# A recurrent section on quarters of the TensorE array: state steps, inside products and turned keys laid out anew

## What is computed

```
state = state * w_t + (state @ a_t) b_t^T + v_t k_t^T      # 64 x 64 per head
y_t   = state @ r_t
```

## Time and profile before

| | |
|---|---|
| median of 3 runs | 2911.92 us (2911.47 to 2911.98) |
| span of the profiled execution | 2909.9 us |
| TensorE busy | 2892.3 us, 99% |
| TensorE weight loads | 2423.8 us, 83% |
| VectorE busy | 1572.7 us, 54% |
| ScalarE busy | 1103.5 us, 38% |
| GpSimd busy | 1584.3 us, 54% |

### The profile page before, as it was taken

One profiled execution on the slowest core, in us unless ns is written; L12 is line 12 of the kernel. 1 busy time (PEld: TensorE's weight loads), 2 busy tenths in 40 slices (PEclk: granted clock), 3 DMA queues, 4 the chain that ended last, 5 costly groups with the idle time before them and its releaser, 6 DMA issues.

```text
span 2909.9 us, 49401 instructions
## 1 busy us (share of the span) xinstructions
PE 2892.3 (99%) x19658; PEld 2423.8 (83%) x19658; DVE 1572.7 (54%) x2227; ACT 1103.5 (38%) x1673; POOL 1584.3 (54%) x1912
## 2 busy tenths in 40 slices
PE   9999999999999999999999999999999999999998
PEld 7877777788888888888888898888898888988887
DVE  5467877524556666775334265445763441473635
ACT  4454434333443322443433343233443342342323
POOL 6432233355646666677444557565584444565654
PEclk9999999999999999999999999999999999999999
DMA  5211111332426777533222323232333222232232
GB/s 173 94 45 41 42 55 45 97 141 95 130 82 217 252 273 254 179 113 126 85 89 73 95 87 113 87 109 87 106 124 115 77 88 87 87 102 94 94 102 73
DMA packets 92292, 322.21 MB, mean 111 GB/s; under 512 B 10144, under 2 KB 14368, under 8 KB 91808
## 3 DMA queue, kind: packets, MB, share of 16 engines
q1 hardware_dynamic: 84544, 302.39, 31.7%
q10 hardware_dynamic: 7520, 16.67, 1.7%
HBM read 315.09 MB, written 3.93 MB: 110 GB/s over the span
## 4 chain that ended last, share of the span: by engine, by line
PE 98%; issue 1%; DVE 1%; POOL 1%; DMA 0%; ACT 0%; POOLq 0%; SPq 0%; ACTq 0%; DVEq 0%
PE bank L906 25%; PE bank L910 25%; PE bank L907 25%; PE bank L1254 2%; PE bank L899 2%; PE bank L901 2%; PE bank L900 2%; PE bank L1265 2%; PE bank L1273 1%; PE bank L934 1%; PE bank L936 1%; PE bank L935 1%; PE bank L958 1%; PE bank L960 1%; PE bank L1785 1%
## 5 line engine op out<-in xcount | busy, mean ns | idle before, releaser
L837 POOL TENSOR_TENSOR w_lo<-w_raw,w_hi 128x256 fp32r<-128x256 f32 x1736 | 1419.2, 852 | 986.9 <-ACT w_hi L1862 980.5
L906 PE MATMUL bank<-act,w_hi 128*128 128x512 f32 (+1 forms) x3464 | 1312.7, 379 | 4.7 <-POOL w_lo L837 2.6
L910 PE MATMUL bank<-act,w_lo 128*128 128x512 f32 (+1 forms) x3464 | 1292.4, 373 | 0.0
L907 PE MATMUL bank<-act,w_hi 128*128 128x512 f32 (+1 forms) x3464 | 1291.4, 373 | 0.0
L906 PEld LDWEIGHTS bank<-act,w_hi 128*128 128x128 f32 x3464 | 652.9, 188 | 126.1 <-issue 8.3
L910 PEld LDWEIGHTS bank<-act,w_lo 128*128 128x128 f32 x3464 | 652.6, 188 | 115.2
L907 PEld LDWEIGHTS bank<-act,w_hi 128*128 128x128 f32 x3464 | 653.4, 189 | 106.7
L1862 ACT CAST w_hi<-w_raw 128x1024 fp32r<-128x1024 f32 (+1 forms) x438 | 454.4, 1043 | 345.1 <-DMA w_raw<-in_weights 163.6
L1870 ACT ACTIVATE arena<-bank 128x512 f32<-128x512 f32 (+1 forms) x177 | 104.3, 593 | 418.2 <-PE bank L910 401.6
L855 POOL TENSOR_TENSOR stats<-stats,exponent 128x8 f32<-128x8 f32 (+2 forms) x38 | 46.6, 1226 | 302.5 <-DVE stats L2914 150.0
L2600 DVE TENSOR_TENSOR act<-tmp,act 128x512 fp32r<-128x512 f32 (+1 forms) x140 | 121.2, 866 | 77.3 <-ACT act L1889 72.7
(11 more groups left out here) (359 smaller groups left out, 3087.4 us busy)
## 6 DMA issues: line engine op xcount, KB each, us to landing
w_raw<-in_weights SPq DMA_DIRECT2D x471, 512.0 KB, 3.5
arena<-in_ada SPq DMA_DIRECT2D x96, 512.0 KB, 5.0
arena<-in_strips ACTq DMA_DIRECT2D x8, 448.0 KB, 3.7
arena<-in_x ACTq DMA_DIRECT2D x1, 2048.0 KB, 10.9
y_scratch<-tmp ACTq DMA_DIRECT2D x7, 256.0 KB, 2.0
arena<-y_scratch ACTq DMA_DIRECT2D x1, 1792.0 KB, 8.1
arena<-in_dft ACTq DMA_DIRECT2D x2, 777.5 KB, 4.2
arena<-in_x SPq DMA_DIRECT2D x3, 512.0 KB, 7.4
```

The lines of the kernel that those rows point to most:

```text
L837: ins = nc.gpsimd.tensor_tensor(w_lo[:, k, cols], weights_of(u)[:, cols], w_hi[:, k, cols].bitcast(F32), ALU.subtract)
L906: nc.tensor.matmul(o, wh, xh, start=first, stop=False)
L907: nc.tensor.matmul(o, wh, xl, start=False, stop=False)
L910: mm = nc.tensor.matmul(o, wl, xh, start=False, stop=last)
```

## The change

The state steps become two 64x64 products, one for each head, on the two diagonal quarters of the array; `MCX` keeps only the two 64x64 maps, and VectorE makes it in one operation. The inside products of the second head go crosswise: what stands in one half of the partitions comes out in the other. The products from the states follow that layout. The turned keys of odd chunks go crosswise too, to a second bank. ScalarE takes both out in three copies (one for what lies straight, two for what lies crosswise), and squares the outputs from their copy.

```diff
-        MCX = take(NC, P)
+        MCX = take(NC, CH)
+        take(NC * CH)
...
             def turned_a(p):
                 o = start_group("tA", p)
-                for c in range(NC):
-                    for rows in HALVES:
-                        mm = nc.tensor.matmul(o[rows, 0, CH * c:CH * (c + 1)], ARs[p % 2][rows, c, 0, :], ident_c[rows],
-                                              start=True, stop=True)
+                for d in range(NC // 2):
+                    for r in range(2):
+                        for h, rows in enumerate(HALVES):
+                            mm = nc.tensor.matmul(o[HALVES[h ^ r], r, CH * d:CH * (d + 1)], ARs[p % 2][rows, 2 * d + r, 0, :],
+                                                  ident_c[rows], start=True, stop=True)
...
             def values_inside(o, p):
                 for d in range(NC // 2):
                     for h in range(2):
-                        for rows in HALVES:
-                            nc.tensor.matmul(o[rows, h, CH * d:CH * (d + 1)], RBB[rows, d, 2 * h, :], TAZ[rows, d, h, CH:P],
-                                             start=d == 0, stop=False, skip_group_check=True)
                         for r, rows in enumerate(HALVES):
-                            mm = nc.tensor.matmul(o[rows, h, CH * d:CH * (d + 1)], MRK[rows, d, h, :], VT_[rows, d, h, :],
-                                                  start=False, stop=2 * d + r == 0, skip_group_check=True)
+                            nc.tensor.matmul(o[HALVES[r ^ h], h, CH * d:CH * (d + 1)], RBB[rows, d, 2 * h, :],
+                                             TAZ[rows, d, h, CH:P], start=d == 0, stop=False, skip_group_check=True)
+                    for h in range(2):
+                        for r, rows in enumerate(HALVES):
+                            mm = nc.tensor.matmul(o[HALVES[r ^ h], h, CH * d:CH * (d + 1)], MRK[rows, d, h, :],
+                                                  VT_[rows, d, h, :], start=False, stop=2 * d + r == 0, skip_group_check=True)
...
             def values_of_states(o, p):
-                                mm = nc.tensor.matmul(o[rows, h, CH * d:CH * (d + 1)], ARs[p % 2][from_rows, c, 1, :],
+                                mm = nc.tensor.matmul(o[HALVES[r ^ h], h, CH * d:CH * (d + 1)], ARs[p % 2][from_rows, c, 1, :],
...
             def scan_step(b, c):
-                    mm = nc.tensor.matmul(b[:, 0, CH * c:CH * (c + 1)], MCX[:, c, :], state(c), start=True, stop=True)
+                    for rows in HALVES:
+                        mm = nc.tensor.matmul(b[rows, 0, CH * c:CH * (c + 1)], MCX[rows, c, :], state(c)[rows], start=True,
+                                              stop=True)
...
             (ScalarE)
-                copied("tA", AZ[:, :, 0, :], one_bank("tA").rearrange("p (c s) -> p c s", s=CH))
+                made(act, "tA", p)
+                o = in_columns("tA", p, CH)
+                nc.scalar.activation(AZ[:, 0:NC:2, 0, :], o[:, 0], ACT.Copy)
+                nc.scalar.activation(AZ[HALVES[0], 1:NC:2, 0, :], o[HALVES[1], 1], ACT.Copy)
+                nc.scalar.activation(AZ[HALVES[1], 1:NC:2, 0, :], o[HALVES[0], 1], ACT.Copy).then_inc(sem("rw_emptied_a"), 1)
...
                 made(act, "Y", p)
-                done(nc.scalar.activation(by_token(YSQ.rearrange("p (d h s) -> p d h s", h=2, s=CH)), in_columns("Y", p, CH),
-                                          ACT.Square), "rw_ysq")
-                copied("Y", by_token(YT.rearrange("p (d h s) -> p d h s", h=2, s=CH)), in_columns("Y", p, CH))
+                y, o = YT.rearrange("p (d h s) -> p d h s", h=2, s=CH), in_columns("Y", p, CH)
+                nc.scalar.activation(y[:, :, 0, :], o[:, 0], ACT.Copy)
+                nc.scalar.activation(y[HALVES[0], :, 1, :], o[HALVES[1], 1], ACT.Copy)
+                nc.scalar.activation(y[HALVES[1], :, 1, :], o[HALVES[0], 1], ACT.Copy).then_inc(sem("rw_emptied_a"), 1)
+                emptied(act, "Y", p)
+                done(nc.scalar.activation(YSQ, YT, ACT.Square), "rw_ysq")
...
             (VectorE)
-            do(V_.memset(MCX, 0.0))
...
-                def state_map(r, signal="vector_step"):
-                    do(V_.tensor_tensor(by_head(MCX[r, :, r]), rm[r, :, :, CH:P], mask(ident_c)[r], ALU.add), signal)
+                def state_map():
+                    do(V_.tensor_tensor(by_head(MCX), rm[:, :, :, CH:P], mask(ident_c), ALU.add), "rw_mcx")
...
-                state_map(HALVES[0])
-                state_map(HALVES[1], "rw_mcx")
+                state_map()
```

More of the change, by code:

```diff
@@ L1308, in values_of_states @@
                     for h, from_rows in enumerate(HALVES):
-                        for r, rows in enumerate(HALVES):
+                        for r in range(2):
                             c = 2 * d + r
                             if c:
-                                mm = nc.tensor.matmul(o[rows, h, CH * d:CH * (d + 1)], ARs[p % 2][from_rows, c, 1, :],
+                                mm = nc.tensor.matmul(o[HALVES[r ^ h], h, CH * d:CH * (d + 1)], ARs[p % 2][from_rows, c, 1, :],
                                                       state(c)[from_rows], start=False, stop=True, skip_group_check=True)
```

## The result

The changed kernel takes 2916.15 us (median of 21 runs, 2915.4 to 2918.5) against 2911.92 (21 runs): ratio 1.0015, 95% interval 1.0009 to 1.002. That is 4.2 us slower, real but inside the 0.2% that was called no difference. The forecast was 2915.5.

The account below looks back on a forecast made before the run. TensorE's own sequence, including shape changes and waits, was taken as the bound (98% of the span). Terms: 0 + 3.7 - 0.1 = +3.6 us on a span of 2909.9, median 2.0 above it: 2915.5 us, range 2907 to 2919.5.

Parts of the forecast that it names:

- Turned keys: Turned keys on TensorE: 0.93 to 0.47 us a pair, but the next group waits for VectorE's L3053, so gain 0.
- if VectorE is no sooner there: Condition on the turned keys in the last pair: their gain is 0 there too unless VectorE's product comes sooner.
- State steps: 48 steps between whole-array products on TensorE: 1.17 us from step to step instead of 0.92, +0.25 each.
- The steps cost no more than now: Rival, chance 0.09: way in and out of quarters hidden, steps stay 0.92 us apart; -4.6 us, 2907.3.
- State map: Two VectorE operations (1.41 us) become one of 0.69, so the first step starts sooner: gain 0.12 us a pair.
- Inside products: Products inside the chunks, 32 records a quarter become 16 on four quarters: 1.86 to 0.93 us a pair.
- the first rival: Quarters sharing a bank don't run together, inside products stay at two quarters' pace: +7.2 us, 2919.1; chance 0.10.
- The wait for b: Next pair's removals wait for VectorE's L2943, queued behind state updates: 0.50 to 0.6 us later, seven pairs, +3.7 us.
- the waits don't bite: Rival, chance 0.07: removals start at 7.27 and turned keys' 0.46 us is earned; -3.7 us, 2908.2.
- ScalarE late with the values: Rival, chance 0.10: ScalarE's three copies delay the group reusing the banks by 0.2 us on seven pairs; 2917.
- time that moves outside this section: Sign of being wrong: all changed code stands in the recurrent section, some 361 us, so time should move only there.

Follow-up runs that it names:

- Steps in columns: The kernel before with each state step as two products of 128 rows by 64 columns, state map as before: 2920.12 us, ratio 1.0029.
- whole steps: The changed kernel with state steps, state map and cleared buffer put back to one whole-array product: 2909.63 us, ratio 0.9992.
- early keys: The changed kernel with VectorE's work for the next pair moved up in its queue: 2910.42 us, ratio 0.9995.
- the last experiment: Whole-array steps, other parts kept, VectorE's next-pair work early in halves, plus one triple of large products moved behind the turned keys: 2905.31 us, ratio 0.9979.

## Why the prediction held

*Turned keys, 0.* Shown, by the changed kernel and by that part alone (2912.15). The cover got shorter and the wait longer, to 0.01 us. The last pair is an exception that the forecast had only as a condition ("if VectorE is no sooner there"): before, L3053 started 0.67 us behind the turned keys instead of 0.32, and the next group came at 1.50. In the changed kernel it comes at 1.15, a gain of 0.35 us. It isn't the shorter turned keys': they alone leave it at 1.51, and the steps alone bring it to 1.16. Why VectorE is late there before stays open.

*State steps, +0.25 each.* Shown: 1.16 instead of the 1.17 worked out from a group's way in and out. That is the distance on TensorE; the forecast set it against the sixth step as it stood, at 5.21, and so had the two distances of 1.00 in its sum, though its text gives 0.92 for all. With the steps alone the recurrence lost 5.8 us and the kernel 6.4; with only them undone the kernel was 6.5 quicker than the changed one. "The steps cost no more than now" is refuted.

*State map, 0.12 a pair.* The first step came at 0.33 behind the large product, as said. Steps in columns, with the same way in but both map operations, start at 0.45.

*Inside products, 1.86 to 0.93.* Measured 0.95 behind whole steps, and 1.02 in the changed kernel, where the sixth step still holds the straight quarters when the first crosswise products start. Four quarters with both row halves writing each bank ran at full pace, 0.058 us a record and quarter, so the first rival falls, and with it, for this case, the Trainium skill's rule that different row tiles can't access one PSUM bank at once ("TensorEngine Tiling (Array Packing)", Restrictions and Gotchas). The term was mis-sized in one small way, the start: on paper they began 0.16 behind the sixth step, in the trace 0.03 (291.58 to 291.61), because the crosswise products find their quarters free and start beside it. With the steps alone, where no inside product goes crosswise, it is 0.17. They began at 6.15 instead of 6.34 and were over at 7.17 instead of 7.27.

*The wait for b, 0.50 to 0.6 on seven pairs.* Shown: 0.57 in pair 1, b ending at 7.59 where 7.63 was worked out, and gone once b moved (early keys). The rival "the waits don't bite" is refuted at both places.

*Behind the removals.* The removals were 0.57 late but the products from the states only 0.52 (8.26 to 8.78): before, the last inside products still held the diagonal quarters while the removals had begun on the others. I had not seen that overlap, and it makes the net loss 0.51 a pair. In pair 6 it was 0.66, and the last pair gained 0.15 where 0.1 was forecast: 6 x 0.51 + 0.66 - 0.15 = 3.6, which was forecast. Between these stretches two more things nearly cancel: 0.24 us that the changed kernel loses ahead of pair 4's steps, between two large products and under no named wait, and the 0.35 that it gains at the last pair's turned keys. The forecast had neither, so that the recurrence's 3.5 lies so near the 3.6 is in part luck; the terms themselves aren't.

*ScalarE late with the values.* The copies took 0.40 us apiece from start to start, not the 0.3 I expected, and held up nothing in the changed kernel: the third was over at 295.69 and L1255 started at 295.96, 0.32 behind the last large product (0.33 before). In the last experiment there are 0.14 us from the end of the third copy (293.24) to the group that it releases (293.38), so the slack here was some 0.1 us.

*What the forecast didn't have.* The kernel is 4.2 us slower, the recurrence 3.5. The forecast named time that moves outside this section as a sign of being wrong, and 0.6 us of it did: the wait of L1622 near 784 us. Two kernels of the nine show it, this one and the steps alone, and these two are also the ones whose median is 0.6 to 0.7 us further above the kernel before than their recurrence (4.2 for 3.5, 6.4 for 5.8); in the others that moved by over 1 us the two agree to 0.3. In both, VectorE's 128x256 operation ahead of L1622 takes 0.91 us and GpSimd's starts 0.04 us behind it; in the other seven it takes 0.35 and GpSimd's starts 0.06 to 0.08 behind. So the slower recurrence seems to have moved two engines onto each other. That the nearness of the starts is the cause isn't shown, since no run shifts only them. The 1.4 us near 2139 go with this one execution, whose time, 2917.19, is 1.0 above the median.

What stays open: this meeting of VectorE and GpSimd, the 0.24 us ahead of pair 4's steps, and VectorE's late start in the last pair of the kernel before.

## To carry to other kernels

Going to smaller tiles, here from two quarters of the array to all four, pays where many products follow one another in the shape (32 inside products: -0.91 us). Going from the whole array to a smaller tile costs where a few products stand between others of the whole array (a step between large products: +0.24 us), even if the array then does less. What such a step costs the kernel is less than that where the step had been waiting for another engine anyway (0.82 us for six). Before speeding up a group, look at what waits behind it: of the three parts, one hid another engine's operation and so was worth nothing, and one needed another engine's queue reordered before it paid. A piece of work that looks like filler may be the cover for a copy; move it and the copy becomes the wait.

## What the runs showed of the hardware

A change of tile shape between whole-array products costs about 0.24 us for both ways together, the same for two 64x64 quarters and for two 128x64 columns: 0.33 instead of 0.24 in, and 0.15 more for the product and the way out. Small fp32 products on quarters that no one uses start 0.03 us behind a product on the others, so the order of issue can hide the start of one group beside the end of another. Each of four quarters takes a record every 0.058 us, with both row halves writing the same bank. A ScalarE copy out of PSUM of half the columns took 0.38 us against 0.60, also on half the partitions: a copy of 64x256 costs what one of 128x256 does.
